# Attention stage of a two-layer decoder step: the next pair's projections in two stretches per query-block group instead of three

## The chip, the core and the metric

The kernel runs on one core of one Trainium2 chip. Its time is the device time of one execution in microseconds (us); lower is better. The engines named here are TensorE (PE in the profile, with PEld for its weight loads), VectorE (DVE), ScalarE (ACT), GpSimd (POOL) and SyncE (SP, which only issues DMAs here).

## What is computed

One step of a two-layer trunk for a prompt of 1024 tokens and 32 sample tokens (8 sequences of 4), 1056 columns together, 1024 channels, everything in float32. Layer 0 mixes by convolutions, layer 1 by dilated attention; each is followed by a convolutional feed-forward part. The change touches layer 1's attention alone:

```
q, k, v = split(rms_norm(h) @ w_qkv)            # 16 heads of 64
for each head, each query i of the prompt:
    s[j] = q_i . k_j / 8 - slope * (i - j) + log(number of branches that read j)
    p = exp(s - max s);  att_i = sum_j p[j] v_j / sum_j p[j]
sample tokens: the same over a cache of 2048 keys, of which 896 are read, and the new ones
y = att @ w_o;  h = h + y
```

The three branches (window, dilation) = (128, 1), (512, 4), (2048, 16) are merged into one softmax by the count in the bias.

## The kernel before

Heads go in eight pairs (`NPAIR`), one after the other. What a pair does on TensorE is written out in `pair(pr)`; `pairs(pair)` calls it for each. Every engine has its own program with the same loops, and the order in each is the order in which the code is written: an engine does one thing after the other, and a wait on a semaphore holds up all that is behind it on that engine.

A pair's eight blocks of 128 queries stand in six groups, `GROUPS = ((7,), (6,), (5,), (4,), (3, 0), (2, 1))`; `g` counts them from 0 to 5. For a group:

- `scores(pr, g)` (L1070) multiplies the queries with the keys, for both heads (`hh` 0 and 1), into the tiles `S` (shown as `reg` and `ob`). It is called one group ahead.
- `neg_scores` on VectorE (L2397) adds the bias and takes the maximum into `neg_s`; ScalarE takes the exponential (L1653); `norm` on VectorE (reciprocal L2408, multiply L2410) scales by the sum. Its last semaphore, `p_ok`, is what TensorE's next step waits for, head by head.
- `turn(g, "lo")` and `turn(g, "hi")` (L1123) transpose the first four blocks of probabilities and the rest into the banks `TP[0]` and `TP[1]`; VectorE (L2418) copies the first head's out into `pT`, ScalarE (L1660) the second's.
- `weigh(g)` (L1137) multiplies `pT` with the values into the output bank.
- `sample_phase(n)` works for the sample tokens, in groups 0, 1, 3 and 4 (`SAMPLE_AT`): phases 1 and 2 are scores (L1180, L1183), which VectorE takes in `sample_scores` (L2428), phases 3 and 4 the product with the values (L1193, L1199), which ScalarE (L1686) and VectorE (L2489) take. All phases write into `TP[0]`.
- Once in a pair there are `turn_values` (L1147, group 0), `turn_weights` (L1157, group 3) and `turn_outputs` (L1165, group 5).

Between these steps stand pieces of the projection of the next pair's queries, keys and values, `filler(f)` with f from 0 to 17 (L1101). A third of the tokens (352 columns) of one of the three is 24 matmuls into the bank `dense`; fillers 2j and 2j+1 are the two halves of third j, 12 matmuls each. A first half waits until `dense` is free (`d_free`), a second half announces that it is full (`d_full`). `next_third(j)` on VectorE (L2450, L2453) scales the third out of the bank into `QT`, `KT` or `VT`. The last pair has no next one: it leaves out the fillers of groups 0, 1 and 2 and does six pieces of the output projection in the others (numbers 9, 10, 12, 13, 15 and 16), of 12, 9, 12, 9, 12 and 9 matmuls.

The weights of the next projection are split in two parts by ScalarE (L514) and GpSimd (L519, a subtraction over 128x1024).

Of the kernel before, what the change touches and what calls it, by code (L numbers as in the profile page):

```python
# [138 lines left out]
def neg_at(g, hh, n):  # L139
    return NEG0[g] + hh * len(GROUPS[g]) + n  # L140
# [71 lines left out]
def build(nc, xT, wstream, par, ident_d, ones_d, stA, stB, stF, kva, kvb, wtab, sbias, cache_k, cache_v,  # L212
# [3 lines left out]
    with ExitStack() as ctx:  # L216
# [567 lines left out]
        def _(pe):  # L784
# [289 lines left out]
            def pair(pr):  # L1074
# [41 lines left out]
                def turn(g, kind):  # L1116

                    blocks = BLOCKS_OF[g][:4] if kind == "lo" else BLOCKS_OF[g][4:]
                    for hh in range(2):
                        pe.wait_ge(p_ok, pr.n(neg_at(g, hh, GROUPS[g].index(blocks[-1][1])) + 1, NNEG))  # L1120
                        (ta_open, tb_open)[hh](kind, g)
                        for i, (off, _, _) in enumerate(blocks):
                            mm = nc.tensor.transpose(TP[hh][:, i * P:(i + 1) * P], neg_s[:, hh, off:off + P], ident[:, :])  # L1123
                        if hh == 0 and g == 1 and kind == "hi":
                            mm = nc.tensor.transpose(TP[0][0:NS, 3 * P:4 * P], VT[:, NP_:T], ident[:, :])
                        mm.then_inc((ta_full, tb_full)[hh], 1)
# [34 lines left out]
                def turn_outputs():  # L1161

                    ta_open("sample")
                    for x in range(2):
                        mm = nc.tensor.transpose(TP[0][:, x * P:(x + 1) * P], so[:, x, :], ident[:, :])  # L1165
                    mm.then_inc(ta_full, 1)
# [36 lines left out]
                for g in range(NGR):  # L1203
                    turn(g, "lo")
                    filler(3 * g)
                    if g == 0:
                        turn_values()
                    if g == 3:
                        turn_weights()
                    if g < NGR - 1:  # L1210
                        scores(pr, g + 1)
                    else:
                        turn_outputs()
                        if not pr.last:
                            pe.wait_ge(d_free, pr.n(9 + 6, 9))
                            scores(Pair(pr.p + 1), 0)
                    turn(g, "hi")
                    filler(3 * g + 1)
                    weigh(g)
                    if g in SAMPLE_AT:  # L1220
                        sample_phase(SAMPLE_AT[g])
                    filler(3 * g + 2)

            pe.wait_ge(d_free, 2 * NT)
            scores(Pair(0), 0)
# [42 lines left out]
            g = NG - 1  # L1268
# [620 lines left out]
        def _(dve):  # L1889
# [511 lines left out]
            def pair(pr):  # L2401
                chain.restart()

                def norm(g, hh):

                    for n, b in enumerate(GROUPS[g]):
                        dve.wait_ge(exp_ok, pr.n(neg_at(g, hh, n) + 1, NNEG))
                        chain(nc.vector.reciprocal(lsum[:, 1, n, hh:hh + 1], lsum[:, 0, n, hh:hh + 1]))  # L2408
                        p = neg_s[:, hh, 512 * n:512 * n + P * (b + 1)]
                        nc.vector.tensor_scalar(p, p, lsum[:, 1, n, hh:hh + 1], None, ALU.mult).then_inc(p_ok, 1)  # L2410

                def turned(g, kind):

                    lo, n = (0, 4) if kind == "lo" else (4, len(BLOCKS_OF[g]) - 4)
                    dve.wait_ge(ta_full, pr.n(ta(kind, g) + 1, NTA))
                    if g == 1 and kind == "hi":
                        nc.vector.tensor_copy(vnew[0:NS, :], TP[0][0:NS, 3 * P:4 * P])
                    nc.vector.tensor_copy(pT[:, 0, lo:lo + n, :],  # L2418
                                          TP[0][:, 0:P * n].rearrange("p (k q) -> p k q", q=P)).then_inc(ta_free, 1)

                def sample_scores(c):

                    lo, n = ((0, 512), (512, NKEYS - 512))[c]
                    dve.wait_ge(ta_full, pr.n(ta("phase", 1 + c) + 1, NTA))
                    if c == 0:
                        dve.wait_ge(sb_in, pr.n(16, 16))
                    settle()
                    nc.vector.tensor_tensor_reduce(out=sps[:, lo:lo + n], in0=TP[0][:, 0:n], in1=sps[:, lo:lo + n],  # L2428
                                                   scale=-1.0, scalar=3.0e38, op0=ALU.add, op1=ALU.min,
                                                   accum_out=snm[:, c:c + 1]).then_inc(ta_free, 1)  # L2430
                    if c == 1:
                        dve.wait_ge(ta_free, pr.n(ta("phase", 2) + 1, NTA))
                        nc.vector.tensor_reduce(snm[:, 2:3], snm[:, 0:2], mybir.AxisListType.X, ALU.min).then_inc(sp_neg, 1)

                def next_third(j):

                    if j < 0:
                        q, x, t = Pair(pr.p - 1), 2, 2
                    else:
                        q, (x, t) = pr, divmod(j, NT)  # L2440
                    if q.last or q.p < 0:
                        return
                    dve.wait_ge(d_full, q.n(9 + 3 * x + t + 1, 9))
                    if x == 1 and t == 0:
                        dve.wait_ge(kt_out, q.n(16, 16))
                    if x == 2 and t == 0:
                        dve.wait_ge(vt_out, q.n(16, 16))
                    dst, r = third((QT[1 - q.par], KT[1 - q.par], VT)[x], t), third(rst, t)
                    if x == 0:
                        ins = nc.vector.scalar_tensor_tensor(out=dst, in0=dense, scalar=HD ** -0.5, in1=r,  # L2450
                                                             op0=ALU.mult, op1=ALU.mult)
                    else:
                        ins = nc.vector.tensor_tensor(dst, dense, r, ALU.mult)  # L2453
                    ins.then_inc(d_free, 1)

                for g in range(NGR):
                    for hh in range(2):
                        norm(g, hh)
                    if g % 2 == 0:
                        next_third(3 * g // 2 - 1)  # L2460
                    turned(g, "lo")
                    if g % 2 == 1:
                        next_third(3 * g // 2)
                    if g == 0:
                        dve.wait_ge(ta_full, pr.n(ta("values") + 1, NTA))
                        nc.vector.tensor_copy(vrow[:, 0:4, :],
                                              TP[0].rearrange("p (t c) -> p t c", c=P)).then_inc(ta_free, 1)
                    if g == 3:
                        dve.wait_ge(ta_full, pr.n(ta("weights") + 1, NTA))
                        nc.vector.tensor_copy(spT[:, 0:4, :],  # L2470
                                              TP[0].rearrange("p (t r) -> p t r", r=P)).then_inc(ta_free, 1)
                    turned(g, "hi")
                    if g < NGR - 1:
                        neg_scores(pr, g + 1)
                    elif not pr.last:
                        neg_scores(Pair(pr.p + 1), 0)
                    if g % 2 == 0:
                        next_third((3 * g + 1) // 2)
                    if g < 2:
                        sample_scores(g)  # L2480
                    if g == 2:
                        dve.wait_ge(sp_exp, pr.n(1, 1))
                        chain(nc.vector.reciprocal(snm[:, 4:5], snm[:, 3:4]))
                        nc.vector.tensor_scalar(sps[:, 0:NKEYS], sps[:, 0:NKEYS], snm[:, 4:5], None,
                                                ALU.mult).then_inc(sp_ok, 1)
                    if g == 4:
                        dve.wait_ge(ta_full, pr.n(ta("phase", 4) + 1, NTA))
                        dve.wait_ge(ta_free, pr.n(ta("phase", 3) + 1, NTA))
                        nc.vector.tensor_tensor(so[:, :, :], TP[0][:, 0:256].rearrange("p (x c) -> p x c", c=P),  # L2489
                                                so[:, :, :], ALU.add).then_inc(ta_free, 1)  # L2490
                    if pr.last and g >= 3:
                        t = g - 3
                        dve.wait_ge(d_full, 9 * NPAIR + t + 1)
                        dve.wait_ge(vt_out, 16 * NPAIR)
                        nc.vector.tensor_copy(third(VT, t), dense).then_inc(d_free, 1)
# [208 lines left out]
```

## Time and profile before

| | |
|---|---|
| median of 3 runs | 2559.16 us (2556.98 to 2563.3) |
| the profiled execution | 2561.66 us, of which 2559.9 us are its span |
| granted TensorE clock over the span | 0.99 |
| TensorE busy | 2496.5 us (98%) |
| VectorE / ScalarE / GpSimd busy | 64% / 31% / 38% |
| attention stage, about | 1150 to 1747 us of the span |

The span runs from the first to the last instruction of the profile. A busy share is an average over stages of different kinds; the attention stage is a row of eight pairs. A granted clock of 1.00 is 2.4 GHz, 0.50 is 1.2 GHz.

### The profile page before, as it was taken

What the parts mean: (1) busy time and instruction counts of PE and PEld (TensorE: products, weight loads), DVE (VectorE), ACT (ScalarE), POOL (GpSimd) and SP (SyncE); (2) the same over time, 40 slices, a digit from 0 to 9 for tenths busy, and PEclk for the clock granted to TensorE, in tenths of its full rate; (3) what the DMA queues carried; (4) which work ended last, traced back from release to release, by engine and by line L of the source; (5) the groups of instructions that cost most, each with busy time, mean ns of one, the idle gap of its engine ahead of it and who ended that gap; (6) DMA issues with size and microseconds to landing.
All of it is one profiled execution on the core that took longest, in us unless ns stands there. A gap on an engine that the chain in (4) does not pass through costs nothing.

```text
span 2559.9 us, 41443 instructions
## 1 busy us (share of the span) xinstructions
PE 2496.5 (98%) x17036; PEld 2375.8 (93%) x17036; DVE 1628.7 (64%) x2409; ACT 804.6 (31%) x1415; POOL 969.6 (38%) x650
## 2 busy tenths in 40 slices
PE   8999998999999999999999999979999999999998
PEld 8989998999999999988888888859999999999998
DVE  6999778666666655565555555554776666665556
ACT  5111344333333211143333334333423333332112
POOL 1000135777777422241011011123277777762223
PEclk9999999999999999999999999989999999999999
DMA  4111102455444544444545454533078777785222
GB/s 148 49 41 36 49 20 62 149 143 145 141 141 141 190 154 134 174 167 142 168 159 162 154 171 148 173 104 124 19 256 286 273 276 274 273 307 193 80 88 86
DMA packets 108667, 383.91 MB, mean 150 GB/s; under 512 B 24000, under 2 KB 44352, under 8 KB 106048
## 3 DMA queue, kind: packets, MB, share of 16 engines
q1 hardware_dynamic: 108480, 381.26, 44.6%
q8 instruction: 136, 2.23, 0.4%
q14 instruction: 51, 0.42, 0.1%
HBM read 339.15 MB, written 176.04 MB: 201 GB/s over the span
## 4 chain that ended last, share of the span: by engine, by line
PE 90%; DVE 5%; issue 1%; POOL 1%; DMA 1%; ACT 1%; DVEq 0%; POOLq 0%; SPq 0%; ACTq 0%
PE reg L976 30%; PE reg L835 19%; PE reg L802 10%; PE reg L1101 10%; PE ob L976 3%; PE reg L1123 3%; PE reg L1070 3%; PE reg L1137 3%; PE reg L908 2%; PE reg L815 2%; PE reg L1041 1%; PE reg L1193 1%; PE reg L1180 1%; PE ob L882 1%; DVE xo L2118 1%
## 5 line engine op out<-in xcount | busy, mean ns | idle before, releaser
L976 PE MATMUL reg<-xo,wq 128*128 128x352 f32 x5280 | 860.9, 323 | 17.7 <-DVE tmp L2197 6.6
L976 PEld LDWEIGHTS reg<-xo,wq 128*128 128x128 f32 x5280 | 850.2, 189 | 22.1 <-DVE tmp L2197 7.2
L835 PE MATMUL reg<-hid,w_sp 128*128 128x352 f32 x3024 | 485.3, 322 | 0.0
L835 PEld LDWEIGHTS reg<-hid,w_sp 128*128 128x128 f32 x3024 | 485.0, 188 | 0.0
L501 POOL TENSOR_TENSOR w_sp<-w_raw,w_sp 128x1024 fp32r<-128x1024 f32 x63 | 175.0, 2780 | 731.1 <-ACT w_sp L496 710.7
L1928 DVE TENSOR_TENSOR h<-reg,h 128x1056 f32<-128x1056 f32 x192 | 241.3, 1257 | 257.7 <-PE reg L835 211.6
L1791 POOL TENSOR_TENSOR wq<-wqr,wq 128x512 fp32r<-128x512 f32 x168 | 239.9, 1437 | 214.7 <-DVE wqr L2157 134.5
L1101 PE MATMUL reg<-xs,w_sp 128*128 128x352 f32 x1575 | 290.3, 334 | 3.8 <-POOL xs L1866 3.8
L1791 POOL TENSOR_TENSOR wq<-w_raw,wq 128x512 fp32r<-128x512 f32 x168 | 266.1, 1596 | 57.3 <-ACT wq L1352 56.6
L1101 PEld LDWEIGHTS reg<-xs,w_sp 128*128 128x128 f32 x1575 | 254.3, 192 | 15.2 <-issue 11.0
L802 PE MATMUL reg<-xs,w_sp 128*128 128x352 f32 x1584 | 253.5, 322 | 0.1
L802 PEld LDWEIGHTS reg<-xs,w_sp 128*128 128x128 f32 x1584 | 252.0, 188 | 1.4 <-issue 1.4
L1352 ACT ACTIVATE wq<-wqr 128x512 fp32r<-128x512 f32 x176 | 110.8, 629 | 422.0 <-DVE wqr L2154 285.5
L519 POOL TENSOR_TENSOR w_sp<-w_raw,w_sp 128x1024 fp32r<-128x1024 f32 x21 | 50.5, 2403 | 452.4 <-ACT w_sp L514 434.4
L496 ACT ACTIVATE w_sp<-w_raw 128x1024 fp32r<-128x1024 f32 x83 | 87.9, 1059 | 424.4 <-PE reg L835 272.7
L2218 DVE SCALAR_TENSOR_TENSOR acc<-g,pt,acc 128x1024 f32<-128x1024 f32 x88 | 184.4, 2096 | 3.1
L2246 DVE TENSOR_TENSOR tmp<-reg,sil 128x352 f32<-128x352 f32 x64 | 31.5, 521 | 178.4 <-POOL sil L1812 178.4
L1660 ACT ACTIVATE pT<-reg 128x512 f32<-128x512 f32 x96 | 47.0, 490 | 246.0 <-PE reg L1123 246.0
L2418 DVE COPY pT<-reg 128x512 f32<-128x512 f32 x96 | 53.2, 555 | 102.4 <-PE reg L1123 101.1
L1352 ACT ACTIVATE wq<-w_raw 128x512 fp32r<-128x512 f32 x176 | 108.8, 622 | 17.0 <-PE reg L802 9.1
L1653 ACT ACTIVATE neg_s<-neg_s,nmx 128x896 f32<-128x896 f32 (+7 forms) x128 | 98.4, 770 | 37.5 <-DVE nmx L2397 36.2
L1123 PE MATMUL reg<-ident,neg_s 128*128 128x128 f32 x576 | 89.8, 285 | 18.2 <-DVE neg_s L2410 16.0
(268 smaller groups left out, 3123.0 us busy)
## 6 DMA issues: line engine op xcount, KB each, us to landing
w_raw<-in_wstream SPq DMA_DIRECT2D x192, 512.0 KB, 4.2
out_sv<-in_cache_v SPq DMA_DIRECT2D x16, 4088.0 KB, 17.0
out_sk<-in_cache_k SPq DMA_DIRECT2D x16, 4088.0 KB, 17.0
kvr<-in_kva SPq DMA_DIRECT2D x16, 2048.0 KB, 9.3
kvr<-in_kvb SPq DMA_DIRECT2D x16, 1536.0 KB, 7.0
hid_spill<-tmp SPq DMA_DIRECT2D x44, 528.0 KB, 5.6
hraw<-hid_spill SPq DMA_DIRECT2D x44, 528.0 KB, 4.5
wt<-in_wtab SPq DMA_DIRECT2D x16, 512.0 KB, 4.0
```

Of the source, the lines that this page charges most:

```text
L496: nc.scalar.activation(w_sp[:, u % 3, 0, :], w_raw[:, u % 3, :], ACT.Copy).then_inc(w_hi, 1)
L501: nc.gpsimd.tensor_tensor(w_sp[:, u % 3, 1, :], w_raw[:, u % 3, :], w_sp[:, u % 3, 0, :].bitcast(F32), ALU.subtract).then_inc(w_lo, 1)
L802: mm = nc.tensor.matmul(out[:, t, :], w[:, wh, k * P:(k + 1) * P], xs[:, xh, k, t * TS:(t + 1) * TS], start=(k == 0 and wh + xh == 0), sto ...
L835: mm = nc.tensor.matmul(out[:, t, :], w[:, wh, kk * 512 + m * P:kk * 512 + (m + 1) * P], hid[:, par_g, kk, xh, t * TS:(t + 1) * TS], start ...
L976: mm = nc.tensor.matmul(out, w[:, wh, k * P:(k + 1) * P], xo[:, o, 1 - xh if o == X_T3 else xh, k, :], start=(first and k == 0 and wh + xh ...
L1101: mm = nc.tensor.matmul(dense, w[:, wh, k * P:(k + 1) * P], xs[:, xh, k, t * TS:(t + 1) * TS], start=(k == 0 and wh + xh == 0), stop=(k == ...
L1123: mm = nc.tensor.transpose(TP[hh][:, i * P:(i + 1) * P], neg_s[:, hh, off:off + P], ident[:, :])
L1352: nc.scalar.activation(wq[:, ring(L, j, q), 0, :], quad_src(L, j, q), ACT.Copy).then_inc(wq_hi, 1)
L1653: nc.scalar.activation(p, p, ACT.Exp, bias=nmx[:, n, hh:hh + 1], scale=-1.0, accum_out=lsum[:, 0, n, hh:hh + 1]).then_inc(exp_ok, 1)
L1791: nc.gpsimd.tensor_tensor(wq[:, r, 1, :], quad_src(L, j, q), wq[:, r, 0, :].bitcast(F32), ALU.subtract).then_inc(wq_lo, 1)
L1928: nc.vector.tensor_tensor(tok(h[:, m, :]), region(r), tok(h[:, m, :]), ALU.add).then_inc(free, 1)
L2218: chain(nc.vector.scalar_tensor_tensor(out=y, in0=g, scalar=w[k], in1=y, op0=ALU.mult, op1=ALU.add))
```

## The change

TensorE's order within a group depends on whether the group's number is even or odd. In an even group the second filler moves from behind the upper transposes to right behind the first filler, and the third moves ahead of the value product. In an odd group the second filler stays, and the third moves from behind the value product and the sample phase to right behind the second. So each group has one stretch of 24 and one of 12 matmuls in place of three of 12, and none stands between the value product (or the sample phase) and the next group's transposes. On VectorE `next_third` of an even group moves ahead of the copy of the upper transposes. Numbers of fillers, their contents and all waits inside them are the same.

```diff
                 for g in range(NGR):
                     turn(g, "lo")
                     filler(3 * g)
+                    if g % 2 == 0:
+                        filler(3 * g + 1)
                     if g == 0:
                         turn_values()
...
                     turn(g, "hi")
-                    filler(3 * g + 1)
+                    if g % 2 == 1:
+                        filler(3 * g + 1)
+                    filler(3 * g + 2)
                     weigh(g)
                     if g in SAMPLE_AT:
                         sample_phase(SAMPLE_AT[g])
-                    filler(3 * g + 2)
...
+                    if g % 2 == 0:
+                        next_third((3 * g + 1) // 2)
                     turned(g, "hi")
                     if g < NGR - 1:
                         neg_scores(pr, g + 1)
                     elif not pr.last:
                         neg_scores(Pair(pr.p + 1), 0)
-                    if g % 2 == 0:
-                        next_third((3 * g + 1) // 2)
```

TensorE, from the upper transposes of group 0 to the first stretch of group 1. `neg_s` are the probabilities, `pT` their transposes, `kvr` the sample cache, `xs` and `w_sp` the projection's operands. A piece like "x16" counts the instructions of one line in a row. Before:

```order
L1123 MATMUL reg<-ident,neg_s 128x128 x8
L1101 MATMUL reg<-xs,w_sp 128x352 x12
L1137 MATMUL reg<-pT,vrow 64x128 x16
L1180 MATMUL reg<-kvr,qb 32x512 x8
L1101 MATMUL reg<-xs,w_sp 128x352 x12
L1123 MATMUL reg<-ident,neg_s 128x128 x8
L1101 MATMUL reg<-xs,w_sp 128x352 x12
```

The same place after the change:

```order
L1123 MATMUL reg<-ident,neg_s 128x128 x8
L1101 MATMUL reg<-xs,w_sp 128x352 x12
L1137 MATMUL reg<-pT,vrow 64x128 x16
L1180 MATMUL reg<-kvr,qb 32x512 x8
L1123 MATMUL reg<-ident,neg_s 128x128 x8
L1101 MATMUL reg<-xs,w_sp 128x352 x12
```

The stretch between the sample scores and the next transposes is gone from here; it stands earlier in the group. The next place on TensorE is from the upper transposes of group 1 to the first stretch of group 2. Before:

```order
L1101 MATMUL reg<-xs,w_sp 128x352 x12
L1137 MATMUL reg<-pT,vrow 64x128 x14
L1180 MATMUL reg<-kvr,qb 32x384 x8
L1183 MATMUL reg<-KT_91,qa 128x32
L1101 MATMUL reg<-xs,w_sp 128x352 x12
L1123 MATMUL reg<-ident,neg_s 128x128 x8
L1101 MATMUL reg<-xs,w_sp 128x352 x12
```

And after:

```order
L1101 MATMUL reg<-xs,w_sp 128x352 x24
L1137 MATMUL reg<-pT,vrow 64x128 x14
L1180 MATMUL reg<-kvr,qb 32x384 x8
L1183 MATMUL reg<-KT_91,qa 128x32
L1123 MATMUL reg<-ident,neg_s 128x128 x8
L1101 MATMUL reg<-xs,w_sp 128x352 x24
```

The stretch behind the sample scores has joined the one ahead of the value product, and the first two of group 2 have become one. VectorE in group 2, from the copy of the lower transposes (`pT` 128x512) to the scaling of the sample softmax (`sps`), before:

```order
L2418 COPY pT<-reg 128x512
L2418 COPY pT<-reg 128x256
L2380 COPY eps<-eps 1x1
L2397 ISA neg_s,nmx<-reg,wt 128x640
L2397 ISA nmx 128x1
L2380 COPY eps<-eps 1x1
L2397 ISA neg_s,nmx<-ob,wt 128x640
L2397 ISA nmx 128x1
L2453 TENSOR_TENSOR KT_93<-reg,rst 128x352
L2483 RECIPROCAL snm<-snm 128x1
L2484 TENSOR_SCALAR sps<-sps,snm 128x928
```

And after, with line numbers that are three higher for the same code:

```order
L2421 COPY pT<-reg 128x512
L2456 TENSOR_TENSOR KT_93<-reg,rst 128x352
L2421 COPY pT<-reg 128x256
L2383 COPY eps<-eps 1x1
L2400 ISA neg_s,nmx<-reg,wt 128x640
L2400 ISA nmx 128x1
L2383 COPY eps<-eps 1x1
L2400 ISA neg_s,nmx<-ob,wt 128x640
L2400 ISA nmx 128x1
L2486 RECIPROCAL snm<-snm 128x1
L2487 TENSOR_SCALAR sps<-sps,snm 128x928
```

The scaling of the projected third (128x352) has moved from behind the two bias steps to ahead of the copy of the upper transposes.

## Rows read from the trace of the kernel before

**Rows 1.** The page: busy time by engine, share of the span, instructions.
```profile
PE 2496.5 (98%) x17036; PEld 2375.8 (93%) x17036; DVE 1628.7 (64%) x2409; ACT 804.6 (31%) x1415; POOL 969.6 (38%) x650
```
**Rows 2.** Stretch of one pair: length, busy time by engine, clock, DMA share, GB/s.
```profile
1229.08:1301.39 72.31, 72.21 (x663) 60.13 (x661) 38.96 (x114) 26.98 (x66) 7.15 (x4) 1.00 0.49 160
```
**Rows 3.** Timeline of TensorE, that pair: start, length, instructions, count.
```profile
1238.44 2.18 PE L1101 MATMUL reg<-xs,w_sp 128*128 128x352 f32 x12
1240.46 1.29 PE L1123 MATMUL reg<-ident,neg_s 128*128 128x128 f32 x8
1241.51 2.15 PE L1101 MATMUL reg<-xs,w_sp 128*128 128x352 f32 x12
...
1251.28 2.18 PE L1101 MATMUL reg<-xs,w_sp 128*128 128x352 f32 x12
...
1254.39 2.18 PE L1101 MATMUL reg<-xs,w_sp 128*128 128x352 f32 x12
...
1258.19 2.17 PE L1101 MATMUL reg<-xs,w_sp 128*128 128x352 f32 x12
1260.29 1.53 PE L1137 MATMUL reg<-pT,vrow 128*64 128x128 f32 x24
...
1264.57 2.17 PE L1101 MATMUL reg<-xs,w_sp 128*128 128x352 f32 x12
...
1272.34 1.95 PE L1193 MATMUL reg<-kvr,spT 128*32 128x128 f32 x64
...
1277.03 2.17 PE L1101 MATMUL reg<-xs,w_sp 128*128 128x352 f32 x12
...
1285.82 2.18 PE L1101 MATMUL reg<-xs,w_sp 128*128 128x352 f32 x12
...
1288.82 2.16 PE L1101 MATMUL reg<-xs,w_sp 128*128 128x352 f32 x12
```
**Rows 4.** Timeline of VectorE behind group 0 (in brackets: idle before, and its releaser).
```profile
1238.58 0.14 DVE L2380 COPY eps<-eps 1x1 f32<-1x1 f32 x1 [2.63 <-PE reg L1180]
...
1240.36 0.69 DVE L2410 TENSOR_SCALAR neg_s<-neg_s,lsum 128x896 f32<-128x896 f32 x1
```
**Rows 5.** Timeline of VectorE behind group 2.
```profile
1260.43 0.52 DVE L2453 TENSOR_TENSOR KT<-reg,rst 128x352 f32<-128x352 f32 x1
...
1261.05 1.71 DVE L2484 TENSOR_SCALAR sps<-sps,snm 128x928 f32<-128x928 f32 x1
...
1263.53 0.56 DVE L2410 TENSOR_SCALAR neg_s<-neg_s,lsum 128x640 f32<-128x640 f32 x1
```
**Rows 6.** Timeline of GpSimd at the same time.
```profile
1259.88 2.39 POOL L519 TENSOR_TENSOR w_sp<-w_raw,w_sp 128x1024 fp32r<-128x1024 f32 x1 [29.81 <-ACT w_sp L514]
```
**Rows 7.** The chain that ended last, in order of time: start, length, what.
```profile
1238.51 2.12 PE reg L1101 x12
...
1246.07 1.93 PE reg L1101 x12
```
**Rows 8.** Timeline of TensorE in the last pair.
```profile
1672.59 1.45 PE L1123 MATMUL reg<-ident,neg_s 128*128 128x128 f32 x8 [2.50 <-DVE neg_s L2410]
...
1683.34 1.39 PE L1123 MATMUL reg<-ident,neg_s 128*128 128x128 f32 x8 [2.71 <-DVE neg_s L2410]
...
1688.29 2.83 PE L1137 MATMUL reg<-pT,vrow 128*64 128x128 f32 x24 [0.56 <-ACT pT L1660]
...
1710.26 1.95 PE L1193 MATMUL reg<-kvr,spT 128*32 128x128 f32 x64
1712.81 1.06 PE L1123 MATMUL reg<-ident,neg_s 128*128 128x128 f32 x8 [0.59 <-ACT so L1686]
1713.62 2.18 PE L1101 MATMUL reg<-xs,w_sp 128*128 128x352 f32 x12
...
1724.79 0.66 PE L1123 MATMUL reg<-ident,neg_s 128*128 128x128 f32 x4 [1.96 <-DVE neg_s L2410]
...
1726.25 3.67 PE L1101 MATMUL reg<-xs,w_sp 128*128 128x352 f32 x12
```

## The prediction

> **What bounds the kernel now.** I read the page first: TensorE is busy for 98% of the span and VectorE for 64% [rows 1]. The change lies in the attention stage alone, in seven pairs of heads out of eight, so next I read one such pair between two equal points of the program. From one turning of the values to the next it takes 72.31 us, TensorE is busy for 72.21 us of them, and the granted clock is 1.00, the 2.4 GHz level [rows 2]. So nothing is idle there that the change could fill. It can gain only what it costs TensorE to pass from one kind of matmul to another, and it can lose by opening a gap that a projection stretch covers now. The timeline of TensorE over that pair shows where the covers are; that of VectorE shows what runs under them.
>
> **What merging is worth.** The change removes no matmul: 216 projections in a pair before and after. In the chain, a stretch of 12 that follows other dense work takes 1.93 us, and one that follows the sample product takes 2.12 us [rows 7]. That 0.19 us is all that a removed stretch can give back. Six stretches go in each of seven pairs, and one in the last: 43 x 0.19 = 8.2 us at most, 0.3% of the time. A measurement of this kernel can tell about 0.3% from no change.
>
> **What the removed cover hides, group by group.** Each of these counts from a fixed event to the start of the next group's first stretch. Wherever that interval stays as it is without the 12 matmuls in it, their 1.93 us [rows 7] is added in full, because they now run elsewhere.
>
> Behind group 0 the sample scores end and the stretch starts at 1238.44; turning begins at 1240.46 and the next stretch at 1241.51 [rows 3]: 3.07 us. Under it VectorE starts at 1238.58, released by the sample scores, and its last scaling of probabilities runs from 1240.36 for 0.69 us, to 1241.05 [rows 4]. The second head's transposes need that, and the next stretch starts 0.46 us later. VectorE therefore sets this interval already, and its order (sample scores first, then the two heads' scaling) is not touched. So: **+1.93 us**. TensorE waits from 1238.5 to 1240.46, some 1.9 us, in place of the stretch.
>
> Behind group 1 the same holds: from 1251.28 to 1254.39 is 3.11 us [rows 3]. The change puts the second stretch ahead of the value product here, so VectorE has more time before the sample scores, but it needs nothing from then. **+1.93 us**.
>
> Behind group 4 it is 1285.82 to 1288.82, 3.00 us [rows 3], with the sum of the two sample products at the head of VectorE's queue. **+1.93 us**.
>
> Behind group 2 there is no sample work. The fixed event is the end of the upper transposes, the stretch at 1258.19; the next group's first stretch starts at 1264.57 [rows 3]. VectorE's last scaling ends at 1263.53 + 0.56 = 1264.09 [rows 5]; with the 0.46 us from above the stretch could not start before 1264.55. The change takes the 0.52 us scaling of a projected third out of this queue and puts it ahead. Is that a gain? The multiply behind it, over 928 columns, takes 1.71 us, while one over 640 takes 0.55 [rows 5]. GpSimd's subtraction runs from 1259.88 for 2.39 us, to 1262.27 [rows 6], across most of the 1.71 us. If the multiply simply sits until GpSimd is done, starting earlier brings nothing: +1.9 us. If it is free to move up, up to the third's own 0.52 us are gained: +1.4 us. I take **+1.9 us**, since GpSimd's start hangs on the same upper transposes and does not move.
> The Trainium skill, page "SBUF — State Buffer", section "Who interferes with whom", says that VectorE in a two-port mode and GpSimd take a shared pair of ports for a whole instruction and that the other "fully blocks". By that rule the sum is the one with 1.9; were there no such lock it would be 7 x 0.5 = 3.5 us less. The 1.71 us agree with the rule.
>
> Behind group 3 probabilities are scaled long before, but the sample product lies in the bank into which the next turning writes, and ScalarE has to copy it first. The last pair has this very order without the stretch: the sample product starts at 1710.26, turning at 1712.81 (0.59 us idle for that copy), the stretch at 1713.62 [rows 8], 3.36 us. Now it is 1272.34 to 1277.03 [rows 3], 4.69 us. 3.36 - 4.69 + 1.93 = **+0.6 us**.
>
> Behind group 5 the scaling is done in time either way, because the merged stretch stands ahead of the value product: the wait stays covered, and I take half of the 0.19 us as gained: **-0.1 us**.
>
> **Sum of the waits.** 3 x 1.93 + 1.9 + 0.6 - 0.1 = 8.2 us for a pair, 57.3 us for seven. In the last pair one stretch of nine leaves its place behind group 4's upper transposes, so the value product waits for their copies: such waits took 0.56 us [rows 8]; with the copies already under way I take 0.4. Together **+57.7 us**. Other queues are not passed: SyncE's order is the same, GpSimd's and ScalarE's too, and each next load of the sample cache is issued by a sample step that then stands at least as far ahead of its use.
>
> **What the clock adds.** No wait of the kind to come is in the seven pairs now; the last pair has three that began at the full clock. After 2.71 us the value product of 24 matmuls took 2.83 us, against 1.53 for the same in a full pair; after 1.96 us a stretch of 12 took 3.67 us against 2.18; after 2.50 us the transposes kept their speed [rows 8, 3]. So two of three such waits were followed by a fall to 1.2 GHz, and a fall cost 3.67 - 2.18 = 1.5 us. The change makes four waits of 1.6 to 1.9 us a pair, 28 in all. The nearest row is the one of 1.96 us, which did fall. 28 x 2/3 x 1.5 = **+28 us**; the bounds are 0 (none falls) and 28 x 1.5 = 42 us.
> The Trainium skill, page "TensorE: Matmul & The Clock Gate", section "A second HAM failure mode: psum-queue depth-cycling", tells of a kernel whose TensorE idles briefly between groups of matmuls and swings between the two levels, paying at every burst. By that rule falls go on in every pair; the last pair's rows agree in two waits of three.
>
> **The total** stands against the profiled execution of 2561.66 us, which lies 2.5 us above the median of the runs: 2561.7 + 57.7 + 28 = 2647.4, and against the median **2645 us**, 3.4% slower.
>
> **Rivals.**
> *The waits come, the clock holds.* The new waits are a little shorter than the 1.96 us one, each has dense projections behind it, and the 2.50 us one did no harm. Then the time is 2559.2 + 57.7 = 2617 us. Chance 0.2.
> *Every wait brings a fall, or more.* 57.7 + 42 = 99.7, 2659 us; beyond that, repeated falls as in the last pair. I give 0.06 to more than 2662.
> *VectorE is not what ends the interval.* The prices at 1.93 us suppose that its queue runs on unchanged from the sample step. If part of it (the 0.69 us scalings, whose input is ready before the sample step) were to run earlier, a wait would shrink to about 0.6 us, as behind group 3, and the sum to between 20 and 45 us: 2580 to 2605. Against it stands the program's order in one queue. Chance 0.08.
> *Only the merging counts (the other side).* If the interval behind the sample step were ended by the transposes on TensorE and not by VectorE, the 12 matmuls would be pure order, no wait would appear, and 43 x 0.19 = 8.2 us would be saved: 2551 us. This decides from the point where VectorE's last scaling ends before the transposes want it; with 1241.05 against a stretch at 1241.51 it is not so. Faster 0.03. That the moved code has no effect on the time, the waits being offset by the merging and by VectorE's earlier third: 0.04 within 0.3%.
> *Forecast:* waits and falls, 2620 to 2662 around 2645: 0.59.
>
> **How the numbers follow.** The range has to take in the forecast and the case without falls; it leaves out the small sums below and the rest above: 2610 to 2662, about 0.8. Faster 0.03, within 0.3% 0.04, slower 0.93.
>
> **What would show it.** TensorE's transposes behind groups 0, 1, 2 and 4 should carry an idle time of 1.5 to 2 us released by VectorE's scaling, and those behind group 3 some 0.6 us released by ScalarE. A pair should last some 80.5 us at the full clock and 84 to 85 with falls as priced. The granted clock over the seven pairs should be 0.92 to 0.97; at 1.00 the clock term is wrong. A pair of under 76 us would mean that VectorE did not bind as read here, and idle times of over 2.5 us that something else, a load or GpSimd, became late.

## The result: 2.9% slower

| | before | after |
|---|---|---|
| median | 2559.96 us (4 runs, 2556.98 to 2563.3) | 2632.22 us (4 runs, 2631.75 to 2638.34) |
| ratio | | 1.0287, 95% interval 1.0267 to 1.0307 |
| profiled execution / span | 2561.66 / 2559.9 us | 2632.06 / 2630.3 us |
| TensorE busy | 98% | 95% |
| granted TensorE clock | 0.99 | 0.985 |

The forecast was +86 us, the result is +72.3 us, inside the range. Of the executions behind the numbers below one is left out, of e7_before_norm_first: it took 5950 us, for a reason that nothing here shows. The page of the kernel after: TensorE does the same number of instructions and has lost three points of its share, and in the list of costly groups its transposes of probabilities (L1123) stand with an idle time ahead of them that was 18.2 us before.

```profile
PE 2511.2 (95%) x17036; PEld 2387.2 (91%) x17036; DVE 1634.7 (62%) x2409; ACT 805.5 (31%) x1415; POOL 970.3 (37%) x650
...
L1123 PE MATMUL reg<-ident,neg_s 128*128 128x128 f32 x576 | 95.0, 292 | 74.4 <-DVE neg_s L2413 67.2
```

Next the busy times by stretch (length, then PE, PEld, DVE, ACT, POOL busy, granted clock, DMA share, GB/s), each from one turning of the values to the next. The first row is a pair without a fall of the clock, the second the one with the most.

```profile
1234.92:1315.44 80.52, 72.60 (x663) 60.06 (x661) 39.41 (x114) 27.11 (x66) 7.15 (x3) 1.00 0.45 144
1315.44:1402.16 86.72, 78.81 (x663) 66.21 (x661) 39.49 (x114) 27.10 (x66) 7.16 (x3) 0.92 0.41 134
```

Against 72.31 us in [rows 2], a pair at the full clock takes 80.52 us: 8.2 us more, with TensorE busy for 72.6 us as before. The second pair is busy for 78.8 us with the same instructions, at a mean clock of 0.92. So the time went two ways: TensorE stands still for longer, and now and then it works at half the clock. The seven pairs as one stretch, of the kernel before and then of the changed one:

```profile
1156.70:1661.70 505.00, 503.88 (x4617) 419.08 (x4615) 272.65 (x798) 188.54 (x462) 47.75 (x21) 1.00 0.49 159
```

```profile
1152.84:1733.46 580.62, 524.83 (x4604) 436.69 (x4603) 276.08 (x798) 189.06 (x461) 47.68 (x20) 0.96 0.43 138
```

The waits of TensorE in the seven full pairs (who waited for whom, us in total, times, longest):

```profile
PE reg L1123 <- DVE neg_s L2413: 49.7, 35, 1.8
PE reg L1123 <- ACT so L1689: 4.2, 7, 0.6
```

Thirty-five waits for VectorE's scaling, five in a pair (behind group 4 both heads wait), and seven for ScalarE's copy. One pair in TensorE's timeline (start, length, instructions, count, idle before and releaser) has them one by one, behind groups 0 to 5:

```profile
1242.42 1.92 PE L1180 MATMUL reg<-kvr,qb 128*32 128x512 f32 x16
1246.14 1.45 PE L1123 MATMUL reg<-ident,neg_s 128*128 128x128 f32 x8 [1.80 <-DVE neg_s L2413]
...
1261.00 1.38 PE L1123 MATMUL reg<-ident,neg_s 128*128 128x128 f32 x8 [1.78 <-DVE neg_s L2413]
...
1267.87 1.36 PE L1101 MATMUL reg<-xs,w_sp 128*128 128x352 f32 x7
...
1269.95 1.53 PE L1137 MATMUL reg<-pT,vrow 128*64 128x128 f32 x24
1273.15 1.32 PE L1123 MATMUL reg<-ident,neg_s 128*128 128x128 f32 x8 [1.67 <-DVE neg_s L2413]
...
1283.93 1.95 PE L1193 MATMUL reg<-kvr,spT 128*32 128x128 f32 x64
1286.48 1.07 PE L1123 MATMUL reg<-ident,neg_s 128*128 128x128 f32 x8 [0.59 <-ACT so L1689]
1287.30 4.06 PE L1101 MATMUL reg<-xs,w_sp 128*128 128x352 f32 x24
...
1299.60 0.66 PE L1123 MATMUL reg<-ident,neg_s 128*128 128x128 f32 x4 [1.53 <-DVE neg_s L2413]
1300.59 0.66 PE L1123 MATMUL reg<-ident,neg_s 128*128 128x128 f32 x4 [0.33 <-DVE neg_s L2413]
...
1310.69 1.09 PE L1123 MATMUL reg<-ident,neg_s 128*128 128x128 f32 x8
```

Behind group 5 there is no wait: there the merged stretch of 24 stands ahead of the value product, and nothing else is late. In the kernel before all these places had a stretch and no idle time ahead of the first transposes; [rows 3] has the one of group 0.

A fall of the clock shows in the next pair. A wait like the others, and then a stretch of 12 at 3.58 us instead of 2.16:

```profile
1326.66 1.72 PE L1123 MATMUL reg<-ident,neg_s 128*128 128x128 f32 x8 [1.79 <-DVE neg_s L2413]
1328.03 3.58 PE L1101 MATMUL reg<-xs,w_sp 128*128 128x352 f32 x12
```

The record of the granted clock has 13 such falls in the seven pairs, and the mean over them is 0.96; before there was none.

### The profile page after: what moved, and what is told of

Same layout as the page of the kernel before. It is cut to its first block, busy times and chain, and to the rows that moved or that the text cites. A ratio compares the mean times of both kernels' runs of the same rounds, so it can differ in the third digit from the quotient of the medians.

```text
span 2630.3 us, 41443 instructions
## 1 busy us (share of the span) xinstructions
PE 2511.2 (95%) x17036; PEld 2387.2 (91%) x17036; DVE 1634.7 (62%) x2409; ACT 805.5 (31%) x1415; POOL 970.3 (37%) x650
## 4 chain that ended last, share of the span: by engine, by line
PE 87%; DVE 8%; issue 2%; POOL 1%; ACT 1%; DMA 1%; DVEq 0%; POOLq 0%; SPq 0%; ACTq 0%
PE reg L976 28%; PE reg L835 18%; PE reg L1101 10%; PE reg L802 10%; PE ob L976 3%; PE reg L1123 3%; PE reg L1070 3%; PE reg L1137 2%; PE reg L908 2%; PE reg L815 2%; DVE neg_s L2413 2%; PE reg L1041 1%; PE reg L1193 1%; PE reg L1180 1%; PE ob L882 1%
## 5 line engine op out<-in xcount | busy, mean ns | idle before, releaser
L1101 PEld LDWEIGHTS reg<-xs,w_sp 128*128 128x128 f32 x1575 | 271.1, 203 | 4.2 <-POOL xs L1869 4.1
L802 PEld LDWEIGHTS reg<-xs,w_sp 128*128 128x128 f32 x1584 | 252.0, 188 | 1.4 <-issue 1.4
L1123 PEld LDWEIGHTS reg<-ident,neg_s 128*128 128x128 f32 x576 | 63.1, 144 | 115.3 <-DVE neg_s L2413 89.5
L1123 PE MATMUL reg<-ident,neg_s 128*128 128x128 f32 x576 | 95.0, 292 | 74.4 <-DVE neg_s L2413 67.2
## 6 DMA issues: line engine op xcount, KB each, us to landing
out_sv<-in_cache_v SPq DMA_DIRECT2D x16, 4088.0 KB, 17.1
```

The costliest lines, as they stand in the source:

```text
L802: mm = nc.tensor.matmul(out[:, t, :], w[:, wh, k * P:(k + 1) * P], xs[:, xh, k, t * TS:(t + 1) * TS], start=(k == 0 and wh + xh == 0), sto ...
L1101: mm = nc.tensor.matmul(dense, w[:, wh, k * P:(k + 1) * P], xs[:, xh, k, t * TS:(t + 1) * TS], start=(k == 0 and wh + xh == 0), stop=(k == ...
```

## Experiments

The theory: in each group a fixed interval, ended by VectorE's queue (behind group 3 by ScalarE's copy), lies under the stretch that was taken away; its matmuls run elsewhere in full, so the price is their 1.93 us per place, less what the queue had to spare. Beside it stand the falls of the clock. Rivals: something else ends the intervals; the clock adds nothing of its own; the price comes with the new order as such. Where the lengths of seven pairs are compared below, they run from the first pair's turning of the values to the last pair's; 505.0 us in the kernel before and 580.6 in the changed one. Kernels that do the even groups' change have one stretch less of 1.93 us in it, since group 0's moved ahead of the first turning. Times of whole executions are coarser than this: the first turning starts between 1148.8 and 1158.2 us in the twelve profiles, though the code ahead of it differs by that one stretch at most.

### VectorE's order turned round: e1_norm_first

```diff
                 for g in range(NGR):
-                    for hh in range(2):
-                        norm(g, hh)
+                    if g - 1 not in (0, 1, 4):
+                        for hh in range(2):
+                            norm(g, hh)
...
+                    if g in (0, 1, 4):
+                        for hh in range(2):
+                            norm(g + 1, hh)
                     if g < 2:
                         sample_scores(g)
```

> The changed kernel, but behind groups 0, 1 and 4 VectorE scales the next group's probabilities before it takes the sample step, not after. Theory (VectorE's queue from the sample step to the last scaling ends the new waits): TensorE then waits only until the sample step's bank is read, so the interval from the end of the sample step to the next stretch falls from 3.1 to about 1.85 us behind group 0, 1.7 behind group 1, 1.4 behind group 4: 4.2 us a pair, 29.6 us in all. The clock should fall some 3 times instead of 13, another 14 us. Expected 2632 - 30 - 14 = 2588 us. Rival (something else, a load or the transposes themselves, ends them): no change, 2632 us.

Measured: 2599.03 us (1.0133 of before, 1.0104 to 1.0163), 33 us less than the change. TensorE's timeline behind group 0:

```profile
1242.60 1.92 PE L1180 MATMUL reg<-kvr,qb 128*32 128x512 f32 x16
1245.62 1.06 PE L1123 MATMUL reg<-ident,neg_s 128*128 128x128 f32 x8 [1.09 <-DVE snm L2431]
```

and its waits in the seven pairs:

```profile
PE reg L1123 <- DVE snm L2431: 14.4, 14, 1.1
PE reg L1123 <- DVE neg_s L2413: 11.6, 7, 1.7
PE reg L1123 <- DVE so L2496: 5.7, 7, 0.8
PE reg L1123 <- ACT so L1689: 4.2, 7, 0.6
```

The releaser has changed from the scaling (`neg_s`) to the reading of the sample step's bank (`snm`, `so`), and the waits behind groups 0, 1 and 4 are 1.09, 0.96 and 0.81 us instead of 1.80, 1.78 and 1.53. Only group 2's, which was not touched, is still 1.66 us; all four falls of the clock that are left followed it. That VectorE's queue ends the intervals is shown, since its order alone was changed. The forecast was 11 us too hopeful. A pair without a fall takes 76.9 us, 3.6 less and not 4.2, which is 4 us of them. And in the last pair, where groups 0 and 1 had waits of 2.50 and 2.69 us, they grew to 3.76 and 3.78, another 2.4. There GpSimd is at work on the output projection's operand, and VectorE's scaling, now earlier, fell under it. VectorE's timeline:

```profile
1708.49 2.52 DVE L2413 TENSOR_SCALAR neg_s<-neg_s,lsum 128x896 f32<-128x896 f32 x1
```

GpSimd's timeline at that time:

```profile
1705.32 5.21 POOL L1869 TENSOR_TENSOR xs<-att,xs 128x1056 fp32r<-128x1056 f32 x2 [3.18 <-ACT xs L1668]
```

2.52 us for a step that takes 0.69 in a full pair.

### Work put into the waits: e2_clock_kept

```diff
                     if g in SAMPLE_AT:
                         sample_phase(SAMPLE_AT[g])
+                    if g in (0, 1, 2, 4) and not pr.last:
+                        for i in range(12):
+                            nc.tensor.transpose(TP[1][:, i % 4 * P:(i % 4 + 1) * P], ident[:, :], ident[:, :])
```

> The changed kernel with 12 extra transposes of the identity, into a bank that is free then, at the start of each wait behind groups 0, 1, 2 and 4 of the seven full pairs: some 1.3 us of TensorE work that nobody reads, inside waits of 1.5 to 1.8 us. Theory (beside the waits, falls of the clock cost 13 x 1.4 = 18 us): the waits stay as long, every pair takes 80.5 us, the granted clock stays at 1.00 and the time is 2614 us. Rival (the falls cost nothing of their own, the 18 us are longer waits): 2632 us or more.

Measured: 2615.23 us (1.0215, 1.0193 to 1.0236). TensorE's timeline behind group 0:

```profile
1239.65 1.92 PE L1180 MATMUL reg<-kvr,qb 128*32 128x512 f32 x16
1241.51 1.53 PE L1228 MATMUL reg<-ident 128*128 128x128 f32 x12
1243.37 1.45 PE L1123 MATMUL reg<-ident,neg_s 128*128 128x128 f32 x8 [0.34 <-DVE neg_s L2416]
```

The seven pairs as one stretch, columns as above:

```profile
1151.70:1711.80 560.10, 544.44 (x4940) 451.98 (x4938) 275.84 (x798) 188.97 (x461) 47.65 (x20) 1.00 0.44 143
```

336 useless transposes were added, and the kernel became 17 us faster. The waits are as long as before, only filled: from the start of the sample scores to the transposes it is 3.72 us in both. The clock stays at 1.00 and a pair takes 80.5 us, every time. This splits the loss cleanly. The waits cost 560.1 + 1.9 - 505.0 = 57.0 us over seven pairs. The falls cost 580.6 - 560.1 = 20.5 us in the profiled execution, 1.6 us each; between the medians of the two kernels lie 17 us.

### The two halves of the change: e3_even_only and e4_odd_only

```diff
-                    filler(3 * g + 2)
+                    if g % 2 == 0:
+                        filler(3 * g + 2)
                     weigh(g)
                     if g in SAMPLE_AT:
                         sample_phase(SAMPLE_AT[g])
+                    if g % 2 == 1:
+                        filler(3 * g + 2)
```

This is the changed kernel with its odd groups as before. The other has the kernel before with `g % 2 == 1` in the first place and `g % 2 == 0` in the second, and VectorE's order of before.

> The change in the even groups alone; odd groups keep their third stretch behind the value product. Theory (each wait has its own price): waits behind groups 0, 2 and 4 stay, 1.93 + 1.9 + 1.93 = 5.8 us a pair, 40 us in all, plus falls at the rate seen (13 in 28 waits, 1.4 us each) 21 x 0.46 x 1.4 = 14 us: 2614 us. Rival (the waits influence each other, so that the odd groups' change makes or hides part of the even groups' price): under 2600 or over 2625 us.

> The change in the odd groups alone. Theory: the wait behind group 1 (1.93 us), the short one behind group 3 for ScalarE's copy (0.6) and the small gain behind group 5 (-0.1) make 2.4 us a pair, 17 us in all, plus 7 x 0.46 x 1.4 = 4.5 us of falls: 2581 us. Rival as for the even groups: under 2572 or over 2592 us.

Measured: 2605.65 us (1.0174, 1.0151 to 1.0198) and 2573.84 us (1.005, 1.0033 to 1.0067). The waits, of the even kernel first and then of the odd one:

```profile
PE reg L1123 <- DVE neg_s L2416: 37.1, 28, 1.8
```

```profile
PE reg L1123 <- DVE neg_s L2413: 12.5, 7, 1.8
PE reg L1123 <- ACT so L1689: 4.2, 7, 0.6
```

37.1 + 12.5 = 49.6, and the whole change had 49.7. The seven pairs took 549.4 and 526.2 us. In the even kernel 1.9 us are added and 4 falls at 1.6 us taken off: its waits cost 549.4 + 1.9 - 505.0 - 6.4 = 39.9 us (forecast 40). In the odd one a pair without a fall takes 74.8 us and the three with one take 76.3, 76.0 and 76.1, so its falls cost 1.5, 1.2 and 1.3 us, and its waits 526.2 - 505.0 - 4.1 = 17.1 us (forecast 17). Together they are the 57.0 us of the whole change: the waits are independent, and each has its price. The falls were off: 4 in 21 waits of the even kernel, where 46% had been expected; the odd one had 3 in 7. Nor do they add up, 4 and 3 against 13 in the same waits of the whole change; with one profile of each kernel, whether that is chance stays open. The odd kernel's median is 7 us under its forecast although its pairs cost what was forecast; in its profile the stage began at 1150.4 us instead of 1156.7.

### GpSimd out of the way: e5_split_later

```diff
+                    if g == 3 and not pr.last:
+                        qkv_hi(act, pr, 2)
                     if g == 2 and not pr.last:
-                        qkv_hi(act, pr, 2)
                         act.wait_ge(d_free, pr.n(9 + 3, 9))
```

> The changed kernel with the split of the value weights (ScalarE L514, GpSimd L519) one group later, so that GpSimd's subtraction no longer runs beside VectorE's multiply of the sample softmax in group 2. Theory (the multiply stands still while GpSimd has the ports): it takes some 0.75 us instead of 1.71, the wait behind group 2 shrinks by about 1 us to 0.7 us, 7 us in all, and its falls go, another 3 to 4 us: 2621 us. Rival (the multiply is slow by itself): still 1.71 us and 2632 us.

Measured: 2613.83 us (1.0205, 1.019 to 1.0221). Behind group 2, in the changed kernel, VectorE's timeline:

```profile
1270.30 2.13 DVE L2487 TENSOR_SCALAR sps<-sps,snm 128x928 f32<-128x928 f32 x1
```

and GpSimd's:

```profile
1269.56 2.37 POOL L519 TENSOR_TENSOR w_sp<-w_raw,w_sp 128x1024 fp32r<-128x1024 f32 x1 [35.25 <-ACT w_sp L514]
```

In the experiment, VectorE's timeline:

```profile
1271.56 0.71 DVE L2488 TENSOR_SCALAR sps<-sps,snm 128x928 f32<-128x928 f32 x1
```

and TensorE's:

```profile
1272.97 1.32 PE L1123 MATMUL reg<-ident,neg_s 128*128 128x128 f32 x8 [0.24 <-DVE neg_s L2414]
```

With the subtraction away the multiply takes 0.71 us, and the wait is 0.24 instead of 1.67. The changed kernel itself says the rest. Counted from the start of the stretch behind the upper transposes (1258.19 in [rows 3], 1267.87 in the pair shown above), the multiply starts after 2.43 us instead of 2.86, because the projected third stands ahead now, and takes 2.13 us instead of 1.71: it ends after 4.56 and 4.57 us. What the change took out of VectorE's queue here, the multiply lost by standing still. The saving is larger than forecast, 18 us and not 11: a pair at the full clock takes 79.0 us, 1.5 less and not 1, since the 0.4 us also come free, and 5 falls are left of 13, where two or three fewer had been expected.

### Half of the cover back: e6_half_behind

```diff
-                    filler(3 * g + 2)
+                    filler(3 * g + 2, 0)
                     weigh(g)
                     if g in SAMPLE_AT:
                         sample_phase(SAMPLE_AT[g])
+                    filler(3 * g + 2, 1)
```

The second argument picks the first or the last 6 of the 12 matmuls, in full pairs.

> The changed kernel with half of the moved third filler, 6 of 12 matmuls, back between the value product or sample phase and the next transposes, in every group of the seven full pairs. Theory (the interval is fixed by VectorE, so matmuls put into it are free until it is full): behind groups 0, 1, 2 and 4 the price halves to 0.96 us, behind group 3 it is gone: 3.85 us a pair, 27 us in all; the idle times of about 0.8 us bring no falls: 2587 us. Rival (the price comes with the order, not with the uncovered length): 2610 us or more.

Measured: 2596.1 us (1.0136, 1.0121 to 1.0151), 9 us above the forecast, with a clock of 1.00 in the full pairs. TensorE's timeline behind group 0 and behind group 2 (this kernel's L1187, L1108, L1130 and L1144 are the sample scores, the projection, the transposes and the value product):

```profile
1239.96 1.92 PE L1187 MATMUL reg<-kvr,qb 128*32 128x512 f32 x16
1241.82 1.23 PE L1108 MATMUL reg<-xs,w_sp 128*128 128x352 f32 x6
1243.68 1.45 PE L1130 MATMUL reg<-ident,neg_s 128*128 128x128 f32 x8 [0.64 <-DVE neg_s L2421]
...
1264.43 1.22 PE L1108 MATMUL reg<-xs,w_sp 128*128 128x352 f32 x6
1265.58 1.53 PE L1144 MATMUL reg<-pT,vrow 128*64 128x128 f32 x24
1267.04 1.23 PE L1108 MATMUL reg<-xs,w_sp 128*128 128x352 f32 x6
1269.72 1.32 PE L1130 MATMUL reg<-ident,neg_s 128*128 128x128 f32 x8 [1.45 <-DVE neg_s L2421]
```

From the start of the sample scores to the transposes it is 3.72 us, the same as without the six matmuls in it. So they are free, and the wait is shorter by their length, as the theory has it. The number for group 2 was wrong. Its interval begins at the upper transposes and holds the piece ahead of the value product as well as the one behind it; 6 and 6 are as much as 12 and none, and its wait stayed at 1.45 us. The forecast had left a price of 3.85 us a pair; with the 0.95 us of group 2 that do not come back it is 4.8, and measured are 77.07 - 72.31 = 4.8 us. That is 7 of the 9 us.

### Both cures on the changed kernel: e8_both_cures

Its edit is that of e1_norm_first and e5_split_later together.

> The changed kernel with both cures: VectorE scales before the sample steps, and the split of the value weights is one group later. If the two act on different waits they add: 2588 - 7 - 4 = 2577 us, no fall of the clock in the seven full pairs. If they act on the same time, it stays near 2588 us.

Measured: 2583.41 us (1.0089, 1.0075 to 1.0103). A full pair takes 75.5 us, 1.4 us less than with the first cure alone, and no clock falls: the two act on different waits. The 6 us above the forecast come from its starting point: it stood on the 2588 us forecast for e1_norm_first, 11 us too hopeful, and the last pair's longer waits, 3.75 and 3.78 us, are here again. The second cure gave more than its 11 us: 16, which are 1.4 us in each of seven pairs and the four falls. Even so repaired, the change costs 3.2 us a pair over [rows 2].

### The same cure on the kernel before: e7, e9 and e10

The edit of e7_before_norm_first is that of e1_norm_first, on the kernel before.

> The kernel before, with VectorE scaling the next group's probabilities before the sample steps of groups 0, 1 and 4. In it TensorE waits between the two heads' transposes there, 0.28, 0.30 and 0.21 us. Theory (VectorE's queue ends these intervals in the kernel before too): they go, 0.8 us a pair, 5.5 us in all: 2554.5 us, 0.2% less. Rival (they are ended by something else): 2560 us.

Measured: 2556.21 us (0.9986, 0.9976 to 0.9996), which is the median of eleven executions. A full pair takes 71.55 us, 0.77 less, as forecast; but in the last pair the waits behind groups 0 and 1 again grew, from 2.50 and 2.71 us to 3.75 and 3.79, which took 2.3 of the 5.2 us back. So the next kernel leaves the last pair's groups 0 and 1 alone:

```diff
+                early = (4,) if pr.last else (0, 1, 4)
                 for g in range(NGR):
+                    if g - 1 not in early:
...
+                    if g in early:
+                        for hh in range(2):
+                            norm(g + 1, hh)
```

> The kernel before with VectorE scaling first behind groups 0, 1 and 4 of the seven full pairs, in the last pair only behind group 4. There GpSimd's subtractions slow the scaling, and with it first the waits behind groups 0 and 1 had grown from 2.50 and 2.71 to 3.75 and 3.79 us. Theory: a full pair takes 71.55 us instead of 72.32 (5.3 us in all), the last pair's waits behind groups 0 and 1 are 2.5 and 2.7 us again, that behind group 4 falls from 1.96 to 0.64 us: 2559.1 - 5.3 - 1.3 = 2552.5 us. Rival (the last pair's order made no difference): 2557 us as with the scaling first in all pairs.

And one more has this in TensorE's program as well:

```diff
                     filler(3 * g + 1)
+                    if g == 5:
+                        filler(3 * g + 2)
                     weigh(g)
                     if g in SAMPLE_AT:
                         sample_phase(SAMPLE_AT[g])
-                    filler(3 * g + 2)
+                    if g < 5:
+                        filler(3 * g + 2)
```

> The same, and in group 5 the third filler joins the second ahead of the value product, the one place where the change should gain. Theory: one stretch start less, 0.1 to 0.19 us a pair and no wait, 1 us in all: a full pair takes 71.4 us, the time is 2551.5 us, which is within what can be told from 2552.5. Rival (the transposes behind group 5 would wait as well): a pair of over 72 us.

Measured: 2551.31 us (0.9976, 0.9964 to 0.9989) and 2549.95 us (0.9963, 0.9949 to 0.9978), against 2556.78 us for the kernel before on the same chip. In both kernels the last pair's waits behind groups 0 and 1 are back at 2.50 and 2.69 to 2.71 us, and the one behind group 4 is 0.63 us instead of 1.96, as forecast. The first kernel is 5.5 us faster than the one before, where 6.6 had been forecast. The seven pairs of e10_group5_merged:

```profile
1148.80:1648.00 499.20, 498.76 (x4617) 419.36 (x4615) 277.26 (x798) 188.19 (x461) 47.67 (x20) 1.00 0.49 161
```

71.50 us a pair, against 71.55 in e9_full_pairs_first: the merging that has no wait under it gains 0.05 us a pair, less than forecast, and the difference of the two medians is no more than the runs differ among themselves. Both kernels beat the one before, by 0.2 to 0.4%.

## Why the prediction was right, and where it was off

**What bounds the kernel** held: with TensorE busy all the time, the change could only open gaps.

**The intervals** held one by one. In the pair that starts at 1234.92, from the start of the last sample matmuls (L1180, L1183, L1199) to the next first stretch, they are 4.93, 3.35 and 3.33 us behind groups 0, 1 and 4, after 4.92, 3.35 and 3.33 in the kernel before, without the stretch in them; behind group 2, from the upper transposes' end, 6.35 us after 6.38; behind group 3, from the sample product to the stretch, 3.37 us where 3.36 had been taken from [rows 8]. The sum was 8.2 us a pair and the pair took 80.52 us, 8.2 more. Over seven pairs 57.3 was forecast and 57.0 measured. In the last pair the value product waited 0.41 us for its copies (0.4).

**Who ends them** held: VectorE's scaling behind 0, 1, 2 and 4, ScalarE's copy behind 3, nothing behind 5; e1_norm_first moved the waits by VectorE's order alone.

**VectorE's moved third** brought nothing behind group 2, the upper of the two values that were weighed; the multiply grew by what the move saved. This trace and e5_split_later show 0.71 us alone, 1.71 and 2.13 beside GpSimd, and an end 0.5 us behind GpSimd's both times. That agrees with the rule of the Trainium skill, page "SBUF — State Buffer", section "Who interferes with whom". Only roughly so: a multiply that had stood still to the end of GpSimd's instruction would have ended 0.7 us behind it, and GpSimd's times in the profile are rough.

**The clock term** was mis-sized, and it carries most of the difference. 28 us were forecast: 28 waits, two in three followed by a fall, 1.5 us each. The price of one was right (1.6). The share was not: 13 of 28 in the profile, 29 of 84 waits of 1.53 to 1.80 us over the change and four experiments (e1, e3, e4 and e5). 17 us between the medians instead of 28 are 11 of the 13.4 us that the forecast of the difference was too high. The rest lies outside the seven pairs: in the profiled executions these cost 57.0 + 20.5 = 77.5 us, while the spans differ by 70.4. Some of it is the last pair, from its turning of the values to its last wait 67.4 us (1733.46 to 1800.86) after 69.1 (1661.74 to 1730.83), at a mean clock of 0.92 after 0.85.

The share had been taken from three waits of one last pair, all of them 1.96 us or longer. It was a draw of three. The changed kernel's last pair has them too, 2.50, 2.69 and 1.97 us long, and none was followed by a fall. The value product behind the second and the stretch behind the third:

```profile
1759.31 1.53 PE L1137 MATMUL reg<-pT,vrow 128*64 128x128 f32 x24 [0.56 <-ACT pT L1663]
...
1797.79 2.16 PE L1101 MATMUL reg<-xs,w_sp 128*128 128x352 f32 x12
```

They had taken 2.83 and 3.67 us in [rows 8]. In the seven profiles that keep these three waits (the kernel before, the changed one, e2 to e6) none, two or all three of them were followed by a fall, 12 of 21. So a count from one execution says little about the next, and what decides whether a wait brings a fall stays open. The range took in every share from no fall to a fall behind each wait, so that it held is no credit to the 28 us.

The rule of the Trainium skill, page "TensorE: Matmul & The Clock Gate", section "A second HAM failure mode: psum-queue depth-cycling", that short idles make the clock swing, agrees with the trace in five pairs of seven; the other two (80.5 us) had the same waits and no fall.

**The merging** was small, as forecast: 0.05 us a pair at the one place where it comes alone, where 0.1 had been put down. (The stretch of 2.12 us in [rows 7] follows the sample scores, and not the sample product as the prediction says.)

## What to carry to other kernels

Filler work on a bound engine is worth what stands under it, and that is read place by place: from the event that starts the other engine's queue to the instruction that waits for its end. Merging fillers saves next to nothing, and moving one out of such an interval costs its full length as soon as the queue ends with no time to spare. Where the bound engine waits at all, look first at the order of the engine it waits for: scaling what is ready before waiting for the next input gave 0.2% here, where every group's moved stretch except group 5's cost time. And the share of waits that bring a fall of the clock cannot be read from three waits of one execution.

## What the runs showed of the hardware

- Waits of the same length, 1.53 to 1.80 us, in the same place of the program were followed by a fall to half the clock in 29 of 84 cases and not in the others; three waits of 1.96 to 2.71 us in the last pair fell none, two or three times by execution (12 of 21 in seven profiles); 42 waits of 0.8 to 1.1 us (e1_norm_first, e8_both_cures) and 7 of 1.45 us (e6_half_behind) were not. A fall cost this kernel 1.2 to 1.6 us.
- Useless work in a gap pays: 336 transposes into the waits made the changed kernel 17 us faster, by the clock alone.
- A VectorE multiply by a column (128x928, float32, in place) took 0.71 us alone, and beside GpSimd's subtraction it ended 0.5 us behind that one whether it had started 0.4 us earlier or not (1.71 and 2.13 us); in the last pair of e1_norm_first 0.69 us (128x896) became 2.52, with an end again 0.5 us behind GpSimd's.
